# The order of 512- and 256-column matrix products in the feed-forward and gated blocks of a two-block transformer

## What is computed

```python
def conv_glu_ffn(h, w_in, conv_w, conv_b, w_out):
    u = h @ w_in
    gate, val = jnp.split(u, 2, axis=-1)
    gate = lax.conv_general_dilated(
        gate, conv_w[:, None, :].astype(gate.dtype), window_strides=(1,),
        padding=((CONV_WIDTH // 2, CONV_WIDTH // 2),),
        dimension_numbers=('NWC', 'WIO', 'NWC'), feature_group_count=D_FF) + conv_b
    return (jax.nn.gelu(gate, approximate=True) * val) @ w_out

def swiglu(x, w_gate, w_up, w_down):
    return (jax.nn.silu(x @ w_gate) * (x @ w_up)) @ w_down
```

## Time and profile before

| | |
|---|---|
| median of 3 runs | 1209.4 us (1207.72 to 1209.48) |
| span of the profiled execution | 1208.0 us |
| mean granted TensorE clock | 0.997 of full speed |
| busy: TensorE products / weight loads | 98% / 86% |
| busy: VectorE / ScalarE / GpSimd | 78% / 55% / 12% |
| DMA | 215.84 MB, mean 179 GB/s |

### The profile page before, as it was taken

One profiled execution on the slowest core, in us unless ns is written; L12 is line 12 of the kernel. 1 busy time (PEld: TensorE's weight loads), 2 busy tenths in 40 slices (PEclk: granted clock), 3 DMA queues, 4 the chain that ended last, 5 costly groups with the idle time before them and its releaser, 6 DMA issues.

```text
span 1208.0 us, 17902 instructions
## 1 busy us (share of the span) xinstructions
PE 1189.8 (98%) x6979; PEld 1038.1 (86%) x6979; DVE 939.8 (78%) x1270; ACT 667.1 (55%) x1060; POOL 150.4 (12%) x275
## 2 busy tenths in 40 slices
PE   8999999999999999999999999999999999999997
PEld 7898888888889988888888988888897888888886
DVE  6767898888776679989887889777775968667765
ACT  5665654444767776544447755434676555444445
POOL 5300510000200012000002100000208420000002
PEclk9999999999999999999999999999999999999999
DMA  7847386555544445665555565655455146565540
GB/s 245 254 154 232 137 269 209 177 196 170 187 151 150 132 149 200 209 206 178 193 170 185 183 230 182 201 178 170 147 175 174 36 156 211 183 209 184 200 140 36
DMA packets 151640, 215.84 MB, mean 179 GB/s; under 512 B 6970, under 2 KB 116924, under 8 KB 151556
## 3 DMA queue, kind: packets, MB, share of 16 engines
q1 hardware_dynamic: 148092, 207.46, 52.2%
q0 software_dynamic: 1760, 3.94, 1.2%
q10 hardware_dynamic: 1704, 3.28, 0.8%
HBM read 213.60 MB, written 1.06 MB: 178 GB/s over the span
## 4 chain that ended last, share of the span: by engine, by line
PE 91%; DVE 4%; ACT 2%; issue 1%; POOL 1%; DMA 0%; POOLq 0%; ACTq 0%; DVEq 0%
PE work L2408 24%; PE work L2411 13%; PE acc L1996 10%; PE acc L1997 9%; PE acc L1998 9%; PE work L1996 5%; PE work L1998 5%; PE work L1997 5%; DVE w_lo L1298 1%; PE work L2397 1%; PE work L2385 1%; PE work L2399 1%; PE work L2018 1%; PE work L2526 1%; PE acc L2053 1%
## 5 line engine op out<-in xcount | busy, mean ns | idle before, releaser
L1298 DVE TENSOR_TENSOR w_lo<-raw,w_hi 128x2048 fp32r<-128x2048 f32 (+1 forms) x194 | 440.7, 2278 | 60.6 <-ACT w_hi L719 60.6
L719 ACT ACTIVATE w_hi<-raw 128x2048 fp32r<-128x2048 f32 (+2 forms) x193 | 365.2, 1898 | 69.5 <-PE work L2411 60.1
L2408 PE MATMUL work<-hT_both,w_hi 128*128 128x512 f32 x1280 | 318.8, 391 | 0.0
L2408 PEld LDWEIGHTS work<-hT_both,w_hi 128*128 128x128 f32 x1280 | 234.8, 188 | 45.2
L2411 PEld LDWEIGHTS work<-hT_both,w_lo 128*128 128x128 f32 x1280 | 174.6, 190 | 12.5
L2411 PE MATMUL work<-hT_both,w_lo 128*128 128x256 f32 x1280 | 178.5, 282 | 0.0
L1996 PE MATMUL acc<-w_hi,aux_hi 128*128 128x512 f32 x400 | 157.8, 395 | 0.0
L1997 PE MATMUL acc<-w_lo,aux_hi 128*128 128x512 f32 x400 | 156.7, 392 | 0.0
L1998 PE MATMUL acc<-w_hi,aux_lo 128*128 128x512 f32 x400 | 155.8, 390 | 0.0
L1085 ACT ACTIVATE aux_hi<-Z 128x256 fp32r<-128x256 f32 x88 | 36.9, 419 | 195.8 <-DVE Z L1722 107.8
L1693 DVE TENSOR_REDUCE Z<-work 128x256 f32<-128x512 f32 x88 | 60.6, 689 | 90.2 <-PE work L2411 88.5
(11 more groups left out here) (271 smaller groups left out, 1782.4 us busy)
## 6 DMA issues: line engine op xcount, KB each, us to landing
raw<-in_ffn_w_in SPq DMA_DIRECT2D x44, 1024.0 KB, 5.2
raw<-in_ffn_w_out SPq DMA_DIRECT2D x22, 1024.0 KB, 5.0
raw<-in_w_gate SPq DMA_DIRECT2D x22, 1024.0 KB, 5.3
raw<-in_w_up SPq DMA_DIRECT2D x22, 1024.0 KB, 5.3
raw<-in_w_down SPq DMA_DIRECT2D x22, 1024.0 KB, 5.0
raw<-in_na_w_qkv SPq DMA_DIRECT2D x12, 1024.0 KB, 7.5
raw<-in_da_w_qkv SPq DMA_DIRECT2D x12, 1024.0 KB, 5.3
raw<-in_ple_w_gate SPq DMA_DIRECT2D x8, 1024.0 KB, 5.0
```

Of the source, the lines that this page charges most:

```text
L719: act.activation(w_hi[:, n % RING, 0:size], raw[:, n % RAW, 0:size], ACT.Copy).then_inc(hi_done, 1)
L1298: dve.tensor_tensor(w_lo[:, n % RING, 0:size], raw[:, n % RAW, 0:size], w_hi[:, n % RING, 0:size].bitcast(F32), ALU.subtract).then_inc(lo_ ...
L2408: pe.matmul(b.rearrange("p (e s) -> p e s", e=2), v[0][:, k, cols(c % 2)], hT_both[:, k, :, :], start=k == 0, stop=False)
```

## The change

In the steps c = 2 to 20 of the four blocks, `up(c)` and `down(c - 2)` become one function, `up_over_down(c)`. It issues the gate's 8 high products, then each of the value's 8 high products followed by one of the gate's 8 low ones, then the 12 down products, the first 8 of them each followed by one of the value's low ones. The step c = 21 keeps `up` and `down`, and `up` is rewritten: within it each low product comes 4 positions (`LAG`) behind its high one, so that the last 4 stand by themselves at the end. High and low halves of a slab are waited for separately, and the low ones later. Number, operands and targets of the products are the same; each bank's sum is formed in another order. `down_done` is raised at the end of `up_over_down` in place of in `down`.

```diff
+LAG = 4
+            def slab_views(n):
+                k, c = slabs[n][1:3]
+                return [r[:, n % RING, 0:k * c].rearrange("p (k n) -> p k n", k=k) for r in (w_hi, w_lo)]
+
             def slab(n):
                 pe.wait_ge(lo_done, n + 1)
-                k, c = slabs[n][1:3]
-                return [r[:, n % RING, 0:k * c].rearrange("p (k n) -> p k n", k=k) for r in (w_hi, w_lo)]
+                return slab_views(n)
...
+                def up_part(ph, c, i, part, k):
+                    g, v = up_bank(ph, c) + i, slab_views(b0 + 3 * (c // 2) - (c >= 2) + i)
+                    d = work[:, g % WORK, :]
+                    if part == 0:
+                        return pe.matmul(d.rearrange("p (e s) -> p e s", e=2), v[0][:, k, cols(c % 2)],
+                                         hT_both[:, k, :, :], start=k == 0, stop=False)
+                    ins = pe.matmul(d[:, 0:S], v[1][:, k, cols(c % 2)], hT_hi[:, k, :], start=False, stop=k == KT - 1)
+                    if k == KT - 1:
+                        ins.then_inc(bank_full[g % WORK], 1)
+                    return ins
+
                 def up(c):
                     g, n = up_bank(ph, c), b0 + 3 * (c // 2) - (c >= 2)
-                    for i in range(2):
-                        v, b = slab(n + i), open_bank(pe, g + i)
-                        for k in range(KT):
-                            pe.matmul(b.rearrange("p (e s) -> p e s", e=2), v[0][:, k, cols(c % 2)], hT_both[:, k, :, :],
-                                      start=k == 0, stop=False)
-                        for k in range(KT):
-                            ins = pe.matmul(b[:, 0:S], v[1][:, k, cols(c % 2)], hT_hi[:, k, :],
-                                            start=False, stop=k == KT - 1)
-                        ins.then_inc(bank_full[(g + i) % WORK], 1)
+                    pe.wait_ge(hi_done, n + 1)
+                    open_bank(pe, g)
+                    for k in range(KT):
+                        up_part(ph, c, 0, 0, k)
+                        if k == LAG:
+                            pe.wait_ge(lo_done, n + 1)
+                        if k >= LAG:
+                            up_part(ph, c, 0, 1, k - LAG)
+                    pe.wait_ge(hi_done, n + 2)
+                    open_bank(pe, g + 1)
+                    for k in range(KT):
+                        up_part(ph, c, 1, 0, k)
+                        if k < LAG:
+                            up_part(ph, c, 0, 1, KT - LAG + k)
+                        if k == LAG:
+                            pe.wait_ge(lo_done, n + 2)
+                        if k >= LAG:
+                            up_part(ph, c, 1, 1, k - LAG)
+                    for k in range(KT - LAG, KT):
+                        up_part(ph, c, 1, 1, k)
+
+                def up_over_down(c):
+                    g, n, e = up_bank(ph, c), b0 + 3 * (c // 2) - (c >= 2), c - 2
+                    pe.wait_ge(hi_done, n + 1)
+                    open_bank(pe, g)
+                    for k in range(KT):
+                        up_part(ph, c, 0, 0, k)
+                    pe.wait_ge(hi_done, n + 2)
+                    open_bank(pe, g + 1)
+                    pe.wait_ge(lo_done, n + 1)
+                    for k in range(KT):
+                        up_part(ph, c, 1, 0, k)
+                        up_part(ph, c, 0, 1, k)
+                    v = slab(b0 + min(3 * (e // 2) + 4, 3 * STEPS - 1))
+                    pe.wait_ge(hid_ready, c0 + e + 1)
+                    for i in range(12):
+                        t, half, part = i // 6, i // 3 % 2, i % 3
+                        ins = pe.matmul(acc[:, 2 * t + half, :], aux[part // 2][:, e % 2, cols(t)],
+                                        v[part % 2][:, e % 2, cols(half, 512)],
+                                        start=e == 0 and part == 0, stop=False)
+                        if i == 0:
+                            pe.wait_ge(lo_done, n + 2)
+                        if i < KT:
+                            up_part(ph, c, 1, 1, i)
+                    ins.then_inc(down_done, 1)
 
                 def down(c, ts=range(T)):
                     v = slab(b0 + min(3 * (c // 2) + 4, 3 * STEPS - 1))
                                 turn_x(ph + 1, 0)
                             ins = product3(acc[:, 2 * t + half, :], both(aux, every, c % 2, cols(t)),
                                            both(v, every, c % 2, cols(half, 512)), c == 0, c == FT - 1)
-                            if c == FT - 1 or (c < FT - 2 and t == 1 and half == 1):
+                            if c == FT - 1 or (c == FT - 3 and t == 1 and half == 1):
                                 ins.then_inc(down_done, 1)
 
                 n = 6 if PHASES[ph - 1] in ("na", "da") else 4
                     if c == 1:
                         second_tile(c)
                     else:
-                        up(c)
-                        down(c - 2)
+                        if c < FT - 1:
+                            up_over_down(c)
+                        else:
+                            up(c)
+                            down(c - 2)
                 for t in range(T):
                     down(FT - 2, [t])
                     down(FT - 1, [t])
```

## The result

| | before | after |
|---|---|---|
| median of 4 runs | 1209.44 us (1207.72 to 1209.55) | 1216.88 us (1216.50 to 1217.91) |
| span of the profiled execution | 1208.0 us | 1215.3 us |
| mean granted clock | 0.997 | 0.997 |

The ratio is 1.0068, 95% interval 1.0054 to 1.0081: slower by 0.7%, where 1198.3 us had been forecast.

The account below looks back on a forecast made before the run. TensorE, busy 98% of the span, was taken as the bound. Product order was to save 11.3 us and block ends to cost 0.2, so 11.1 us off 1209.4 gave 1198.3 us, range 1196.5 to 1210.5.

Parts of the forecast that it names:

- Part 1: Order of TensorE products in the four blocks: a long-short pair falls from 349 to 340 ns, saving 11.3 us.
- My upper bound: Costliest price considered for a long-short pair: 120 for the 256 and 233 for the 512 behind it, 353 ns.
- the lower end: Cheapest price for a long-short pair, 113.3 + 226.7 = 340.0 ns, taken as the forecast.
- The last steps: Step c = 21 of each block: about 0.10 us saved a step, 0.4 us for four.
- Part 2: Banks, waits and slabs in ordinary steps: gate and value complete 1.7 us later, at no cost.
- The margin of 2.8 us: Time by which the down slab is ready before the next step's down products want it; it was 5.6.
- Rival D: Later banks make TensorE wait at the down products, 0.1 us a step, 7.6 us given back, 1206 us; chance 0.07.
- Part 3: End of the two convolution blocks: a later gate delays the last hidden tile, 0.1 us each, 0.2 us lost.
- A: Rival: price goes by width alone, 346.7 ns a pair, 2.9 us saved, 1206.5 us; chance 0.21.
- B: Rival: the loss is spread over the 512s between lone 256s, a pair stays at 349 ns, 1209.4 us; chance 0.16.
- C: Rival: slower, late loads make a pair 353.3 ns, 5.4 us more, 1214.8 us; chance 0.13.
- the mixer's first interval: Profile row in the mixer where a 256 follows a 512: 0.11 us, read as nothing being late yet.

Follow-up runs that it names:

- e4: Changed kernel with most 256-column products left out in three blocks, and groups of two long and two short in the fourth; fourth-block step 8.293 us.
- e5: Changed kernel with 64-column loads, by block, for short (order of before), short, long and all products; steps 8.240, 8.340, 8.220, 8.247 us.
- e9: Changed kernel, short products 320, 384, 448 columns with 64-column loads in three blocks; in the fourth 256, long products' loads 112; pairs 375.7, 403.3, 430.0, 340 ns.
- e7: Kernel with all 16 short products in one run (e3), but c = 20 of the convolution blocks in the order of before; 1207.85 us, ratio 0.9990 to before.
- e8: Changed kernel with c = 20 and 21 of all four blocks in the order of before; 1213.84 us, ratio 1.0042 to before.
- e11: Changed kernel reordered: short products in four runs of four, two long between runs, convolution blocks' last two steps as before; 1206.48 us, ratio 0.9976 to before.
- e6: Changed kernel with full loads and short products made 320, 384, 448 and 128 columns wide by block; pairs 380.0, 406.5, 437.3, 340.0 ns.
- e10: Changed kernel regrouped by block in c = 2 to 19, long and short: 4 and 4, 3 and 3, 2 and 4, 1 and 2; steps 8.353, 8.360, 8.267, 8.300 us.
- e12: Changed kernel reordered to two runs of eight short products, with 2, 1, 3 long or 2 down products between, by block; steps 8.280, 8.293, 8.293, 8.280 us.
- e3: Changed kernel reordered to collect all 16 short products in one run, c = 21 as before; 1210.09 us, ratio 1.0007 to before.

## Why the prediction was wrong

**Part 1, the price of a pair, failed, and it alone turned the sign.** The step that failed is the sentence that a short product costs 113 between long ones *and* "the long product that comes next has its load ready long before". The first half held: the interval from a lone 256 to the next product is 0.113 in e4 and in the first pair of each three after. The second half looked at the wrong place. The load that must pass during the 256 is the one of the 512 behind it; it wants about 120 and has 113. Make that load shorter, and the settled pairs fall to 340.0 (64 columns in e5, 112 in e9). The 512 pays, 233 to 241 instead of 226.7. The earlier trace rows can't show this: the product behind their first 256 is another short one, which pays in the same way and was read as the price of "its like". My upper bound, 353 ns, was computed for a late load, and its sum is the measured 353.3. That it fits to the nanosecond is partly luck: the bound was 120 + 233, and what came is 113 + 233, 117 + 241 and 120 + 236 in turn, 116.7 + 236.7 on average. And e5's second block shows that lateness of the 512's load alone isn't the whole of it, since shorter loads of the 256s bring the pair to 347. I took the lower end because its row was the nearest; but a pair has two intervals, and that row showed only one of them. The forecast step was 8.160 us and the measured one is 8.387: 16 x 0.0133 = 0.213 from the pairs and 0.013 behind the last of them. Over 76 steps that is 17.2 us, which turns 11 us of saving into 6 us of loss.

**The last steps** were to gain 0.4 and lost 0.2, by the same price.

**Part 2 held.** Gate and value complete 1.9 us later (4.63 and 7.46 us into the step instead of 2.76 and 5.56; 1.7 forecast), and no ordinary step waits: no idle time in the groups. The margin of 2.8 us, half of what it was, sufficed. Rival D is refuted.

**Part 3 had the right mechanism with a wrong size**, 0.87 us for each of two blocks where 0.1 was booked. I moved ScalarE's slab work by 0.87, the delay of the gate of c = 21. Measured against TensorE's product before the last tile's, that slab work ended 1.52 us ahead of it before (306.82 against 308.57 - 0.23 = 308.34) and 0.19 behind it after (305.94 + 1.90 = 307.84 against 307.65): 1.71, not 0.87. The reason is on VectorE. 302.95, the sum of c = 21's gate, comes straight behind slab work of 300.75 to 303.03, which is queued behind the work on c = 20, whose gate was 1.9 us later. Before, the same two stand here:

```profile
299.72 2.28 DVE L1298 TENSOR_TENSOR w_lo<-raw,w_hi 128x2048 fp32r<-128x2048 f32 x1
301.93 0.68 DVE L1693 TENSOR_REDUCE Z<-work 128x256 f32<-128x512 f32 x1
```

Against TensorE's product the sum stood 308.34 - 301.93 = 6.41 us ahead, and now 307.65 - 302.95 = 4.70: the same 1.71. In these steps VectorE starts not when the bank that it sums is full but when what is queued before it is done, and that carries the delay of the step before. e7 shows it by putting c = 20 back (e8 puts c = 21 back as well).

**The rivals.** A's price, 346.7, isn't the one found in alternation, and its reason fell with e5; yet a price by width is what e11 reaches (4 short and 2 long), so order can be free, but only in that pattern. The Trainium skill, "TensorE: Matmul & The Clock Gate", "Back-to-back issue gap", gives its formula by width alone for isolated products and says that in a stream of loads and products both set the spacing. I had used the formula for a stream. These runs bear out the second half, and it has no figure for them: orders of one and the same 28 + 16 products take from 8.267 to 8.387 us. B, the spread loss, was near in kind (e6 shows it at 320 to 448 columns) and short in size. C was right in sign and sum, and in the main in its cause, a late load, if not in how the 353.3 divides: 8.37 a step where 8.387 came, and 1214.8 us; what is above it is part 3 (1.7) and the exit (1.0), less what the stretches outside gave. Against C stood that nothing is late in the mixer's first interval. It was true and said nothing of the second interval.

## What to carry to other kernels

Price a pattern, not an instruction: when the profile shows one interval of a pair, the other is unknown, and its bound should be taken as seriously as the neat end. A product shorter than the weight load that must pass beside it (here 113 against some 120 ns) delays the product *behind* it; try such products in few long runs or, here better, in fours with two long ones between, and measure. When a bank's completion moves, follow each engine's queue from the previous step on, and look at the last steps of a block, where a margin that the loop always has is gone.

## What was not expected of the hardware

- One late load costs more than its lateness. Behind a lone 256 the load misses by about 7 ns, and the five 512s behind it take 27 ns more than five undisturbed ones, always in the intervals 233, 236, 228, 233, 231 within 1 or 2 ns (e4), and the same behind runs of 8 and 16.
- Shorter loads didn't always help. Nine 512s in a row, eight of them with 64-column loads, stand 230 ns apart and not 226.7 (e5, third block; 229 with 112 columns in e9).
- The price depends on the grouping and not monotonically. Over the floor of 8.267 us: 0.000 with fours and two long between (e10, e11), 0.013 with eights and two between (e12), 0.020 with one run (e3), 0.026 with 2 and 2 (e4) and with eights and one or three between (e12), 0.033 with pairs and one between (e10), 0.040 before, 0.086 with 4 and 4, 0.093 with 3 and 3 (e10), 0.120 in full alternation.
- A 128-column product beside a 512 costs as much as 256 columns should: 340.0 ns a pair, 60 and 280, and not 283 (e6).
- 320 to 448 columns in alternation with 512 lose 10 to 12 ns a pair although their loads have time, and 64-column loads give back less than two thirds of it (e6, e9). This, why short loads of the 256s alone bring a pair from 353 to 347, and why the fours are free, stays open.
